# Latent attention with tokens on partitions: row sums on VectorE, rope by addressing, heads turned by TensorE

## The reference, cut to what matters

```python
c_q, c_kv, k_r, q_d, k_d, v_d = jnp.split(h @ w_in[l], split_at, axis=-1)     # 384, 256, 32, 512, 512, 512
q = (rmsnorm(c_q, g_cq) @ w_uq).reshape(B, S, 8, 96)
kv = (rmsnorm(c_kv, g_ckv) @ w_ukv).reshape(B, S, 8, 128)
k_nope, v = kv[..., :64], kv[..., 64:]
k = jnp.concatenate([k_nope, broadcast(k_r)], axis=-1)         # 64 of the head, 32 shared by all heads
q, k = rmsnorm(q, g_qn), rmsnorm(k, g_kn)                      # over the 96
q, k = rope on the last 32 of each (halves of 16, angle = position * inv_freq)
o = softmax(q k^T / sqrt(96)) v                                # 8 heads
```

## Time and profile before

| | |
|---|---|
| median of three runs | 1646.68 us |
| the profiled execution's own time | 1644.55 us |
| its span (first to last instruction) | 1642.8 us |
| granted TensorE clock, mean over the span | 0.995 |
| PE, DVE, ACT, POOL busy | 97%, 69%, 56%, 8% |
| second block, layer 0: start of `turned(0)` to start of `turned(15)` | 1043.31 to 1114.36 us |
| the same, layer 1 | 1369.86 to 1440.92 us |

### The profile page before, as it was taken

One profiled execution on the slowest core, in us unless ns is written; L12 is line 12 of the kernel. 1 busy time (PEld: TensorE's weight loads), 2 busy tenths in 40 slices (PEclk: granted clock), 3 DMA queues, 4 the chain that ended last, 5 costly groups with the idle time before them and its releaser, 6 DMA issues. The chain is left out here.

```text
span 1642.8 us, 31046 instructions
## 1 busy us (share of the span) xinstructions
PE 1589.0 (97%) x12874; PEld 1463.2 (89%) x12874; DVE 1129.8 (69%) x1763; ACT 919.0 (56%) x1459; POOL 127.2 (8%) x106
## 2 busy tenths in 40 slices
PE   6999999999999999999999999999999999999999
PEld 3987478999999999966899999878999998799999
DVE  2799677645566655897765556778887567788873
ACT  3444756545365444647554446767666467676662
POOL 0230000112001100300011000000101000001110
PEclk9999999999999999999999999999999999999999
DMA  9443666656546555435566653323555533245553
GB/s 395 160 152 131 258 236 227 235 216 240 192 167 221 205 188 201 155 125 207 195 228 237 220 184 119 118 78 130 207 191 202 204 112 116 77 137 200 207 193 118
DMA packets 46172, 303.36 MB, mean 185 GB/s; under 512 B 5072, under 2 KB 7376, under 8 KB 12752
## 3 DMA queue, kind: packets, MB, share of 16 engines
q1 hardware_dynamic: 45312, 299.78, 50.7%
q0 software_dynamic: 288, 0.92, 0.1%
q10 hardware_dynamic: 432, 0.68, 0.1%
HBM read 298.22 MB, written 3.15 MB: 183 GB/s over the span
## 5 line engine op out<-in xcount | busy, mean ns | idle before, releaser
L2002 DVE TENSOR_TENSOR wl<-raw,wh 128x1040 fp32r<-128x1040 f32 (+1 forms) x472 | 576.4, 1260 | 295.8 <-ACT wh L1759 229.9
L1759 ACT ACTIVATE wh<-raw 128x1040 fp32r<-128x1040 f32 (+1 forms) x472 | 466.5, 1031 | 195.5 <-PE bank L1552 109.3
L1547 PE MATMUL bank<-hx_hi,wh 128*128 128x256 f32 x1856 | 519.6, 280 | 6.0 <-ACT hx_hi L1759 3.8
L1552 PE MATMUL bank<-hx_lo,wh 128*128 128x256 f32 x1856 | 516.2, 278 | 0.0
L1550 PE MATMUL bank<-hx_hi,wl 128*128 128x256 f32 x1856 | 514.7, 277 | 0.3 <-DVE wl L2002 0.2
L1547 PEld LDWEIGHTS bank<-hx_hi,wh 128*128 128x128 f32 x1856 | 349.0, 188 | 10.8 <-issue 9.8
L1550 PEld LDWEIGHTS bank<-hx_hi,wl 128*128 128x128 f32 x1856 | 349.1, 188 | 2.8 <-issue 1.7
L1552 PEld LDWEIGHTS bank<-hx_lo,wh 128*128 128x128 f32 x1856 | 348.8, 188 | 1.0 <-DVE hx_lo L1995 0.4
L1550 PE MATMUL bank<-hid_hi,wl 128*128 128x256 f32 x912 | 252.2, 277 | 1.4 <-DVE wl L2002 1.4
L1547 PE MATMUL bank<-hid_hi,wh 128*128 128x256 f32 x912 | 252.5, 277 | 0.3 <-ACT wh L1759 0.2
L1552 PE MATMUL bank<-hid_lo,wh 128*128 128x256 f32 x912 | 251.9, 276 | 0.0
(11 more groups left out here) (218 smaller groups left out, 1891.5 us busy)
## 6 DMA issues: line engine op xcount, KB each, us to landing
raw<-in_wts SPq DMA_DIRECT2D x208, 1032.0 KB, 4.9
raw<-in_wts SPq DMA_DIRECT2D x50, 1024.0 KB, 6.6
raw<-in_wts SPq DMA_DIRECT2D x20, 776.0 KB, 4.3
raw<-in_wts SPq DMA_DIRECT2D x4, 584.0 KB, 4.4
tscr<-tmp SPq DMA_DIRECT2D x4, 512.0 KB, 7.4
bias<-tscr SPq DMA_DIRECT2D x4, 512.0 KB, 6.0
raw<-in_wts SPq DMA_DIRECT2D x2, 648.0 KB, 4.0
xTc<-in_ctxT SPq DMA_DIRECT2D x1, 1024.0 KB, 10.6
```

What stands on the lines that cost most here:

```text
L1547: pe.matmul(out, block(f, M.wh, w0 + k, ncols, c, m), x_hi, start=first and k == 0 and o == 0, stop=False, skip_group_check=True)
L1552: ins = pe.matmul(out, block(f, M.wh, w0 + k, ncols, c, m), x_lo, start=False, stop=last and k == nk - 1, skip_group_check=True)
L1759: return act.activation(out, in_, func, bias=bias, scale=scale)
L2002: tt(M.wl[k][:, cols], M.raw[r][:, cols], M.wh[k][:, cols].bitcast(F32), ALU.subtract).then_inc(*on.inc(lo))
```

## The change

The latent queries and keys are made with tokens on partitions (128 tokens of a block `tb` by the features of several heads):

- `queries(u)`: u = 2j + tb; four heads of one token block with 9 products (stationary: 128 tokens of the latent; moving: 384 columns of weights). ScalarE squares all 384 columns and copies the 64 plain features of each head. VectorE, at once and in the same step, applies rope to the 32 others (four small operations: `rope_on`, which exchanges the halves by addressing) and sums the squares of each head (`tensor_reduce`). In the rest (`qn2`) ScalarE makes the inverse root of 128x4, TensorE turns four heads (four transposes), ScalarE copies 96x512 with the gain.
- `keys(tb, f)`: all 8 heads of one token block with 6 products of 512 columns; ScalarE squares; VectorE sums by head and adds the shared part `kss`, at once. In the rest (`scale`, "mla_k2") ScalarE makes the root of 128x8 and VectorE scales into two buffers (four operations); this puts a second rest (`turn`, "mla_k3") at the end of the pending ones: eight transposes and two ScalarE copies of 96x512.
- The shared key part is turned (two transposes) instead of multiplied with `swap2`, gets its rope with `rope_on`, and its squares are summed once. Its two ScalarE squares of 32x512 and a GpSimd memset go.
- Cosine and sine become rows of 32 per token times gain (`rt`), made from 32 columns instead of 256 by `tables`, and by 12 small VectorE operations in `rope_rows`; two small loads change.
- The weights of "ukv" are reordered on the host so that keys and values stand together; the piece is done when `K0`, `K1` and `V` are all planned. `BETWEEN` is rewritten.

```diff
-BETWEEN = ("h r D0 h L0 L2 N r r D2 D4 r D3", "", "D1 r r Q0", "K0", "", "s K1 h s V Q1", "r r", "s r D5 h h", "h r",
-           "Q3 Q2 h", "", "s K2 r r r K3 h", "s", "r O0 h O1 s", "", "O2", "", "h O3 h", "h", "h s T0 T1 T2 T3 h")
+BETWEEN = ("h r D0 h L0 L2 N r r D2 D4 r D3", "", "D1 r r Q0", "Q1", "K0 s r", "s K1 h V r", "r r", "s r r D5 h h", "h",
+           "Q2 Q3 h", "r", "s r O0 h", "s O1", "h", "", "O2", "", "h O3 h", "h", "h s T0 T1 T2 T3 h")
...
+    def mla_q(f, tb, b, free, cq_toks, t):                               # TensorE
+        out, sl = b.t[:, 0:384], slice(P * tb, P * tb + P)
+        on.wait_ge(free)
+        for k in range(3):
...
+            mm(out, M.cqn[0][:, k, sl], block(f, M.wh, k, 384, 0, 384), k == 0, False)
...
+    def heads_turned(o, y):
+        for i in range(4):
+            ins = pe.transpose(o.t[0:96, P * i:P * i + P], y.t[:, 96 * i:96 * i + 96], M.ident)
+        return ins
...
+    def mla_kv(f, c0, tb, b, ck_toks):
+        sl = slice(P * tb, P * tb + P)
+        for k in range(2):
+            c = slice(1024 * k + c0, 1024 * k + c0 + 512)
+            on.wait_ge(f["thi"][k], f["tlo"][k], ck_toks[k])
+            mm(b.t[:, :], M.ckn[0][:, k, sl], M.wh[f["k"]][:, c], k == 0, False)
+            mm(b.t[:, :], M.ckn[0][:, k, sl], M.wl[f["k"]][:, c], False, False)
+            ins = mm(b.t[:, :], M.ckn[1][:, k, sl], M.wh[f["k"]][:, c], False, k == 1)
+        return ins
...
+    def qn1(b, tok, sq, sq_free, y, y_free, t_sq, t_y, **_):             # ScalarE
+        on.wait_ge(tok, sq_free)
+        fn(sq.t[:, 0:384], b.t[:, 0:384], ACT.Square).then_inc(*on.inc(t_sq))
+        on.wait_ge(y_free)
+        heads = lambda x: x[:, 0:384].rearrange("p (h c) -> p h c", c=96)[:, :, 0:64]
+        fn(heads(y.t), heads(b.t), ACT.Copy).then_inc(*on.inc(t_y))
...
+    def rope_on(dst, w, src, C, S, t):                                   # VectorE
+        tt(w[0], src, C, ALU.mult).then_inc(*on.inc(t[0]))
+        tt(w[1][:, :, 0:16], src[:, :, 16:32], S[:, :, 0:16], ALU.mult).then_inc(*on.inc(t[1]))
+        tt(w[1][:, :, 16:32], src[:, :, 0:16], S[:, :, 16:32], ALU.mult).then_inc(*on.inc(t[2]))
+        on.wait_ge(t[2])
+        tt(dst, w[0], w[1], ALU.add).then_inc(*on.inc(t[3]))
+
+    def qn1(l, j, tb, b, sq, y, t_tab, qs_free, t_sq, t_y, t_d, **_):
+        heads = lambda x: x[:, 0:384].rearrange("p (h c) -> p h c", c=96)
+        w = [x.t[:, 384:512].rearrange("p (h c) -> p h c", c=32) for x in (y, sq)]
+        C, S = (M.rt[:, l, 0, i, tb, :].unsqueeze(1).to_broadcast([P, 4, 32]) for i in range(2))
+        on.wait_ge(t_sq, t_y, t_tab)
+        rope_on(heads(y.t)[:, :, 64:96], w, heads(b.t)[:, :, 64:96], C, S, t_d)
+        on.wait_ge(qs_free)
+        dve.tensor_reduce(M.qs[:, 8 * j:8 * j + 8].rearrange("p (h t) -> p h t", t=2)[:, :, tb], heads(sq.t), AXX,
+                          ALU.add).then_inc(*on.inc(t_d[4]))
...
+    def mla_k1(tb, sq, d, d_free, t_krr, t_sq, t_d, **_):
+        on.wait_ge(t_sq, d_free)
+        dve.tensor_reduce(d.t[:, :], sq.t[:, :].rearrange("p (h c) -> p h c", c=64), AXX, ALU.add).then_inc(*on.inc(t_d[0]))
+        on.wait_ge(t_d[0], t_krr)
+        ts(d.t[:, :], d.t[:, :], M.kss[:, tb:tb + 1], ALU.add).then_inc(*on.inc(t_d[1]))
+
+    def mla_k2(tb, b, d, ys, y_free, t_krr, t_r, t_y, **_):
+        on.wait_ge(t_r, t_krr)
+        for i in range(2):
...
+            tt(y[:, :, 0:64], b.t[:, T * i:T * i + T].rearrange("p (h c) -> p h c", c=64), r.to_broadcast([P, 4, 64]),
+               ALU.mult).then_inc(*on.inc(t_y[2 * i]))
+            tt(y[:, :, 64:96], M.krt[:, tb, :].unsqueeze(1).to_broadcast([P, 4, 32]), r.to_broadcast([P, 4, 32]),
+               ALU.mult).then_inc(*on.inc(t_y[2 * i + 1]))
```

More of the change, by code:

```diff
@@ L85, in shape_constants @@
     c["swap1"] = j1
[L86 to L91, removed]
+    sq = np.concatenate([c[k] for k in ("ident", "ones", "bones", "swap1")], axis=1)
     t = np.arange(T)
@@ L1149, in tables @@
         t, t_l = ev("mm"), ev("tab")
-        t_d = [ev("tab") for _ in range(18)]
+        t_d = [ev("tab") for _ in range(19)]
         t_sin = [ev("sin"), ev("sin")]
@@ L1156, in tables, with rope_rows @@
         small["t_l"] = t_l
-        tmps.give(small["rb"], t_d[0], t)
-        tmps.give(angb, t_d[-1])
         tmps.give(kb, t_d[-1])
-        t_rope[:] = [t_sin[1]]
+        small.update(ang=angb, t_sin=t_sin, t=t)
+    def rope_rows():
+        t_g = [ev("tab") for _ in range(12)]
+        step("rope_rows", ang=small["ang"], rb=small["rb"], t_sin=small["t_sin"], t_rw=small["t_rw"], b1_free=b1_free,
+             t_g=t_g)
+        tmps.give(small["rb"], t_g[-1], small["t"])
+        tmps.give(small["ang"], t_g[-1])
+        t_rope[:] = [t_g[-1]]
     def copy_out(i):
@@ L1281, in lora_norm @@
             pending.append(rest)
-        q_toks, k_toks, v_toks, qs_toks = [], [], [], []
+        q_toks, k_toks, v_toks, qs_toks = [[], []], [[], []], [], [[], []]
         uq = []
[L1287 to L1303, removed]
-            def rest():
[L1306 to L1318, removed]
+        def queries(u):
+            j, tb = u // 2, u % 2
+            if tb == 0:
+                uq[:] = [take(("uq", l, j), look=False)]
+            b, t = banks.get(), ev("mm")
+            step("mla_q", f=uq[0], tb=tb, b=b, free=b.free, cq_toks=cq_toks, t=t)
+            if tb:
+                p.done(uq[0], t)
+            sq, y = tmps.get(), tmps.get()
+            t_sq, t_y, t_d = ev("hsq"), ev("hxg"), [ev("rope") for _ in range(5)]
+            step("qn1", l=l, j=j, tb=tb, b=b, tok=t, sq=sq, sq_free=sq.free, y=y, y_free=y.free, t_tab=list(t_rope),
+                 qs_free=list(qs_free), t_sq=t_sq, t_y=t_y, t_d=t_d)
+            banks.give(b, t_y, t_d[2])
+            tmps.give(sq, t_d[4])
+            def rest():
+                o, t_t, t_ln, t_rs, x = banks.get(), ev("mm"), ev("ln"), ev("rs"), ev("q2")
+                step("qn2", l=l, j=j, tb=tb, y=y, ready=[t_y, t_d[3]], t_sum=t_d[4], o=o, free=o.free, rf=rf, t=t_t,
+                     t_ln=t_ln, t_rs=t_rs, x=x)
+                tmps.give(y, t_t)
+                banks.give(o, x)
+                q_toks[j].append(x)
+                qs_toks[j].append(t_rs)
+            pending.append(rest)
@@ L1429, in dil_out, with latent @@
             p.gemm(bk_f[0], 4, 512, bk[-1], H["c"], mix_toks, k0=4, last=False, done=i == 1)
-        def lat_keys(hp):
-            if hp == 0:
+        n_kv = []
+        def latent(part):
+            if not ukv:
                 ukv.append(take(("ukv", l), look=False))
-            k_part(hp, ukv[0])
+            t = mla_values(ukv[0]) if part == "V" else keys(int(part), ukv[0])
+            n_kv.append(t)
+            if len(n_kv) == 3:
+                p.done(ukv[0], t)
         bk_f, nrm, final = [], Norm(s), [None]
@@ L1456, in rest @@
                 pending.pop(0)()
-        portion = {"r": rest, "s": p.one, "h": p.one_half, "V": lambda: mla_values(ukv[0])}
+        portion = {"r": rest, "s": p.one, "h": p.one_half, "V": lambda: latent("V")}
         portion.update({f"D{j}": (lambda j=j: hfree.update(x=[dil_piece(j)])) for j in range(6)})
```

297 lines of the change are left out of this document (148 added, 149 removed).

## The result

The changed kernel takes 1663.6 us (median of 4 runs, 1662.2 to 1664.9) against 1647.4 for the kernel before beside it (1646.5 to 1648.2): a ratio of 1.010, interval 1.0084 to 1.0116. The forecast was 1655.5. The direction was right, the size about half (8.8 us longer forecast, 16.2 measured).

The account below looks back on a forecast made before the run. PE bounds most of the kernel; from turned(0) to turned(15) PE, DVE and ACT are coupled. There +9.0 for two layers, constants' load -0.2: +8.8 on the profiled 1644.55, hence 1653.4, or 1655.5 against the median; range 1650 to 1661.

Parts of the forecast that it names:

- TensorE's savings: Fewer query, key, sum and swap instructions on TensorE: 176 records fewer, 25.0 us of work, 12.5 a layer.
- VectorE and ScalarE keep their load: turned(0) to turned(15): savings of about 4 and 3 us offset by earlier `out2` splits; about 51 and 50 us stay.
- The walk: Queues followed through one layer, turned(0) to turned(15): weights queue behind `qn1`, keys and splits; 76.4 us long, +9.0 for two layers.
- its sign: Check on the walk's splits: wrong if ACT shows fewer than five weight pieces between turned(3) and turned(12).
- The clock: Rival, chance 0.18: after PE's waits between turned(1) and turned(12) the grant falls, up to twice a layer; 1662 us.
- nine stands of 1 to 4.4 us: TensorE's waits in the walk, at turned(1), (3) to (6), (8) and (10) to (12); longest 4.4 at turned(6).
- the shorter `Q0`, shared key and constants: Small gains: `Q0` products 0.6 shorter, shared key's exchange 0.3 back, constants' load -0.2.
- The rival's four falls: Size of the clock rival: four falls of the grant, 1.7 us each where PE bounds, +6.8 on the forecast: 1662.
- PE bounds everywhere: Rival, chance 0.13: TensorE limits the whole kernel, so its savings count in full, -25.0 - 0.2: 1621.5 us.
- The coupling costs as before: Rival, chance 0.27: the turned(0) to turned(15) stretch stays at 70 to 71 us; 1635 to 1648, centre 1644.

Follow-up runs that it names:

- fill_exact: Changed kernel plus extra identity transposes where TensorE stood, thinned to leave out turned(4), and 16 ahead of the scores of latent heads 4 and 5: 1658.2 us, ratio 1.0072.
- defer_late: Changed kernel with VectorE's part of `qn1` listed one piece later and the `out2` splits where they stood before the change: 1643.6 us, ratio 0.9979 to the kernel before.
- gate_moved: Changed kernel with the two half splits into the slot that `D5` frees listed one piece later, ahead of turned(6)'s values: 1656.3 us, ratio 1.0051.
- fill_after: Changed kernel with the first, thickest filling: extra identity transposes ahead of the waits for weights at nine turns: 1663.8 us, ratio 1.0097.
- tuned3_fill: `defer_late` with row sums waiting only for the layer before and `Q2`, `Q3` portions relisted, plus 11, 7, 14 identity transposes at turned(1), (3), (9): 1642.5 us.

## Why the prediction was right in direction and wrong in size

1. **TensorE's savings: right, and worth nothing by themselves.** 176 instructions fewer, as forecast. The products of 384 columns start 0.17 to 0.18 apart at full clock (1085.02 to 1085.20), against 0.170 taken. In the stretch TensorE's busy share is 83%, above the 70 to 80% forecast: at the low grant the same products are busy for longer.
2. **VectorE and ScalarE keep their load: right.** 50.9 and 50.6 us against "about 51 and 50". By form, VectorE's new operations (count, busy, mean ns) have the lengths taken from the earlier trace rows, 0.29, 0.22 and 0.56:

```profile
L2104 DVE TENSOR_TENSOR tmp<-bank,rt 128x128 f32<-128x128 f32 x4 | 1.2, 292 | 3.4 <-ACT tmp L1774 3.4
L2105 DVE TENSOR_TENSOR tmp<-bank,rt 128x64 f32<-128x64 f32 x4 | 0.9, 214 | 0.0
...
L2117 DVE TENSOR_REDUCE qs<-tmp 128x4 f32<-128x384 f32 x4 | 2.2, 544 | 0.0
```

3. **The walk: right in its sum.** It gave 76.4 us for the stretch; with the clock held it measures 77.0 and 76.6. Most of the named stands were there, smaller: 3.1 us forecast at turned(1), 2.68 measured; 4.4 at turned(6), 2.19 measured (and 0.9 just ahead of it); 2.4 and 1.35 at turned(8); 2.0 and 1.95 at the scores ahead of turned(10); 2.0 and 1.95 at turned(11). Of 3.2 at turned(4), 1.30 and 0.56 stood ahead of it; of 1.8 at turned(3), 0.27. At turned(5) and turned(12) there was none: ahead of turned(5) `D5` covers more than I walked. Some of this is luck: the step from turned(5) to turned(6) was walked at 7.6 us and takes 6.5, the two before it were walked too short, and the errors cancel. ScalarE shows nine half splits between turned(3) and turned(12), 4.5 pieces where the walk named five as its sign.
4. **The clock: the step that failed.** The prediction set the fall of the clock beside the sum, as a rival at 0.18 ("it decides if the grant falls at all between `turned(1)` and `turned(12)`"), and summed at full clock a walk with nine stands of 1 to 4.4 us. So the sum had nothing for a slow clock. It fell five times a layer, for 20.5 us. By `fill_exact` that is 2.8 and 3.1 us a layer, 5.9 together, of the 7.4 by which the measured change (16.2) exceeds the forecast one (8.8); in the medians it is 5.4 (1663.6 less 1658.2). The rest is small: the walk is 0.6 and 0.2 short, and I had credited 1.9 us to the shorter `Q0`, shared key and constants, where 17.4 less 16.2 leaves 1.2 for all that lies outside the stretches. (The kernel before ran 0.7 higher this time, which makes the 7.4 the 8.1 between 1655.5 and 1663.6.) The result is outside the 1650 to 1661 that the prediction gave the walk, and just inside the 1632 to 1664 that took in the clock. The rival's four falls at 1.7 us each gave 1662, close to the result, but not by its terms: ten spells at some 0.6 each. Most of a slow spell costs nothing, which fits its lying beside work of VectorE and ScalarE.
5. **The rival "PE bounds everywhere"** falls: 12.5 us less of TensorE's work a layer, by the prediction's count, and the stretch is 8.7 longer. **"The coupling costs as before"** falls too, for this list; `defer_late` shows that it was one list away.
6. The Trainium skill, page "TensorE: Matmul & The Clock Gate", section "Why this matters for your kernels", warns of idle gaps between bursts of products. The runs agree that such gaps bring the clock down, and show it for gaps shorter than the page has in view: the grant fell behind stands of 1.3 to 2.7 us, and with the stands filled it hardly fell. The Trainium skill, page "Perfetto Trace Analysis", section "Identifying the Most-Contended Engine", says to work on the engine with the highest occupancy first. Read on the whole kernel (weight loads 89%) that pointed to TensorE and to the rival that fell; read on the stretch (76, 73, 70%) it puts no engine far ahead, and there the runs agree: the same operations in another order took 20 us less.

## What to carry to other kernels

When a change takes work from the engine that covers the others, walk the queues of all engines step by step; the savings by operation say nothing. Ask of each new item in an engine's list what it waits for and whose work stands behind it: two half splits behind a slot not yet free cost 4.1 us a layer (1.6 of them by the slow clock that came with it), and listed one piece later, with the same work, they gave this back. If the walk itself gives TensorE stands of a few us where it had none, put the slow clock into the sum, for the part of the products that others wait for: here 2.8 to 3.1 us a layer for 20.5 us at half clock. And try the freed slots' and the new portions' place in the list before judging the operations: here they were slower by 1.0% in one order and faster by 0.3% in another.

## What the runs showed of the hardware

- The grant went to 0.50 while TensorE was 100% busy, shortly after stands of only 1.3 to 2.7 us before it. Not every stand was followed by a fall: behind the one of 1.35 at turned(8) the next products ran at 1.00, and so they did behind the one of 0.59 in `gate_moved`.
- Transposes of a constant, 0.11 us each (33 in the 3.66 us ahead of turned(6) in `fill_after`), kept it up: 0.87 became 0.96 and 0.98 in `fill_exact`. Whether that gains time is another question: 2.8 and 3.1 us a layer there, nothing in `tuned3_fill`.
- 20.5 us a layer at half clock cost about 3 us in the changed kernel, not the 10 that the same products would take longer if nothing else ran beside them (an estimate: half of 20.5).
